# A two-block network on one core: the first norm's transfers, angles and table loads put in another order

## The reference, cut to what matters

```python
def layer_norm(x, g, b):
    xf = x.astype(jnp.float32)
    mu = jnp.mean(xf, axis=-1, keepdims=True)
    var = jnp.mean(jnp.square(xf - mu), axis=-1, keepdims=True)
    return ((xf - mu) * lax.rsqrt(var + EPS) * g.astype(jnp.float32) + b.astype(jnp.float32)).astype(x.dtype)

def rope_tables(positions):
    inv = ROPE_BASE ** (-jnp.arange(0, MLA_ROPE, 2, dtype=jnp.float32) / MLA_ROPE)
    ang = positions.astype(jnp.float32)[..., None] * inv
    return jnp.cos(ang), jnp.sin(ang)

def first_block(x, positions, ln_in_g, ln_in_b, w_in, ...):
    cos, sin = rope_tables(positions)
    h = layer_norm(x, ln_in_g, ln_in_b)
    for l in range(DEPTH):
        mix = token_mixers(h, cos, sin, w_in[l], ...)
        ...
```

## Time and profile before

| what | value |
|---|---|
| median of 3 runs | 3002.48 us |
| profiled execution, own time | 3005.76 us |
| its span in the profile | 3003.8 us |
| TensorE busy | 2892.7 us (96%) |
| VectorE busy | 1781.0 us (59%) |
| ScalarE busy | 1444.2 us (48%) |
| GpSimd busy | 1127.0 us (38%) |
| granted TensorE clock, mean | 0.991 |

### The profile page before, as it was taken

How to read it: one execution, slowest core, us unless ns; L and a number is a source line. 1 busy time by engine, 2 the same in 40 slices (tenths; PEclk the granted TensorE clock), 3 DMA queues, 4 the chain that set the end, 5 groups by cost and what they waited for, 6 DMA issues and landing times.

```text
span 3003.8 us, 45876 instructions
## 1 busy us (share of the span) xinstructions
PE 2892.7 (96%) x13808; PEld 2341.6 (78%) x13808; DVE 1781.0 (59%) x2643; ACT 1444.2 (48%) x2178; POOL 1127.0 (38%) x667
## 2 busy tenths in 40 slices
PE   6999999999999999999999998999999999989998
PEld 5777888887778888877877877888768877877886
DVE  4785444035865442158644268999566643379997
ACT  3544555225554553212445135888323453238886
POOL 2323444543232444555643531111556444601102
PEclk9999999999999999999999998999999999999999
DMA  4213333532122334434322357999633222459997
GB/s 130 71 43 92 98 93 96 174 90 79 43 96 77 96 95 139 145 108 107 105 71 57 92 181 266 396 411 402 158 101 113 75 64 76 151 188 374 409 411 240
DMA packets 374724, 466.55 MB, mean 155 GB/s; under 512 B 31334, under 2 KB 278176, under 8 KB 374496
## 3 DMA queue, kind: packets, MB, share of 16 engines
q1 hardware_dynamic: 349712, 391.52, 38.6%
q0 software_dynamic: 14944, 53.01, 5.4%
q10 hardware_dynamic: 9840, 19.29, 2.2%
HBM read 423.09 MB, written 33.55 MB: 152 GB/s over the span
## 4 chain that ended last, share of the span: by engine, by line
PE 58%; issue 22%; POOL 9%; DVE 6%; ACT 2%; ACTq 1%; DMA 1%; POOLq 0%; DVEq 0%; SPq 0%
PE bank L489 8%; PE bank L490 8%; POOL unit_lo L409 7%; PE bank L2207 4%; PE bank L2360 3%; PE bank L2361 3%; PE bank L2364 3%; PE bank L848 2%; PE bank L2374 2%; PE bank L2375 2%; PE bank L2378 2%; PE bank L1037 2%; PE bank L953 1%; PE bank L956 1%; PE bank L954 1%
## 5 line engine op out<-in xcount | busy, mean ns | idle before, releaser
L409 POOL TENSOR_TENSOR unit_lo<-unit_raw,unit_hi 128x1024 fp32r<-128x1024 f32 (+1 forms) x186 | 444.9, 2395 | 738.6 <-ACT unit_hi L402 738.6
L489 PE MATMUL bank<-xT_hi,unit_hi 128*128 128x512 f32 (+1 forms) x1776 | 689.5, 392 | 8.1 <-DVE d_lo L2875 3.7
L490 PE MATMUL bank<-xT_lo,unit_hi 128*128 128x512 f32 (+1 forms) x1776 | 667.2, 380 | 0.0
L489 PEld LDWEIGHTS bank<-xT_hi,unit_hi 128*128 128x128 f32 x1776 | 335.8, 189 | 95.7 <-issue 26.0
L490 PEld LDWEIGHTS bank<-xT_lo,unit_hi 128*128 128x128 f32 x1776 | 336.2, 189 | 64.5 <-issue 5.6
L402 ACT ACTIVATE unit_hi<-unit_raw 128x1024 fp32r<-128x1024 f32 (+1 forms) x186 | 194.8, 1047 | 367.0 <-PE bank L848 152.9
L394 POOL TENSOR_TENSOR unit_lo<-unit_raw,unit_hi 128x1024 fp32r<-128x1024 f32 (+2 forms) x158 | 325.3, 2059 | 13.2
L392 POOL TENSOR_SCALAR unit_hi<-unit_raw 128x1024 fp32r<-128x1024 f32 (+2 forms) x158 | 150.3, 951 | 459.6 <-PE bank L2207 269.4
L474 DVE TENSOR_TENSOR wt_lo<-wt,wt_hi 128x1024 fp32r<-128x1024 f32 x192 | 238.5, 1269 | 33.8 <-ACT wt_hi L469 33.0
L848 PE MATMUL bank<-xT_hi,unit_lo 128*128 128x512 f32 x976 | 241.2, 389 | 0.0
L474 DVE TENSOR_TENSOR xT_lo<-wt,xT_hi 128x1024 fp32r<-128x1024 f32 x192 | 233.1, 1219 | 8.3 <-ACT xT_hi L469 0.8
(11 more groups left out here) (585 smaller groups left out, 6206.2 us busy)
## 6 DMA issues: line engine op xcount, KB each, us to landing
wt<-in_w SPq DMA_DIRECT2D x384, 512.0 KB, 7.2
unit_raw<-in_w_in SPq DMA_DIRECT2D x272, 256.0 KB, 3.1
unit_raw<-in_w_ffn_up SPq DMA_DIRECT2D x176, 256.0 KB, 3.1
unit_raw<-in_w_ffn_down SPq DMA_DIRECT2D x88, 256.0 KB, 3.0
unit_raw<-in_w_out SPq DMA_DIRECT2D x64, 256.0 KB, 2.8
y_rows<-yb POOLq DMA_DIRECT2D x28, 512.0 KB, 7.1
y_rows<-zeros POOLq DMA_DIRECT2D x24, 512.0 KB, 5.2
unit_raw<-in_w_br SPq DMA_DIRECT2D x96, 128.0 KB, 2.3
```

The source lines that it names most:

```text
L409: pool.eng.tensor_tensor(lo, raw, hi.bitcast(F32), SUB).then_inc(self.split, 1)
L489: pe.matmul(out, wh, xh, start=first, stop=False)
L490: pe.matmul(out, wh, xl, start=False, stop=False)
```

## The change

On SyncE's queue, row tile 0 comes first, then g and b, then tile 1, the bulk of `konst`, the turning matrix, and tiles 2 and 3. The positions and the frequencies move to ScalarE's queue. The angles are computed by GpSimd instead of VectorE, with instructions of one or two inputs (12 of them, each waiting for the one before). ScalarE takes the square root of a constant first, which loads the square root's table. The sine stands behind the high part of tile 0 and the tables behind the high part of tile 1 in ScalarE's list. TensorE's list is the same.

```diff
@@ -100,7 +100,7 @@
     "ld_turn": (2, 0, 0),
     "ld_x": (1, 0, 0),
     "tab_mm": (4, 0, 0),
-    "tab_ev": (4, 0, 0),
+    "tab_ev": (5, 0, 0),
     "h_st": (0, 0, 4),
     "ov_wt": (0, 0, 48),
     "ov_x": (0, 0, 8),
@@ -108,7 +108,7 @@
     "ov_read": (0, 0, 32),
     "ov_val": (0, 0, 128),
     "ov_begin": (2, 0, 16),
-    "set_up": (7, 0, 0),
+    "set_up": (18, 0, 0),
     "y_zero": (0, 12, 0),
     "xb_ld": (0, 0, 16),
     "y_st": (0, 0, 14),
@@ -187,7 +187,7 @@
     "h_hi": (0, 0, 17),
     "y_ev": (0, 0, 33),
     "gt_use": (0, 0, 26),
-    "v_step": (24, 236, 342),
+    "v_step": (16, 236, 342),
     "norm_var": (4, 8, 8),
     "norm_z": (4, 8, 8),
     "norm_lo": (8, 16, 16),
@@ -778,13 +778,12 @@
                 high(NT - 1)
                 return
             deviation(0)
-            beside[0]()
             for i in range(NT):
                 if i + 1 < NT:
                     deviation(i + 1)
                 high(i)
-                if i == 1:
-                    beside[1]()
+                if i < 2:
+                    beside[i]()
 
         LAST = -NT
 
@@ -3157,17 +3156,13 @@
 
         def loads0(E):
             sp = E.eng
-            posi = proj[0:N_ANGLES, 0, :].bitcast(I32)
-            for rows, name in ((slice(0, 32), "positions"), (slice(32, N_ANGLES), "positions_2")):
-                sp.dma_start(posi[rows, :], over(t[name], [rows.stop - rows.start, S])).then_inc(ld.sem, ld.up(E))
-            sp.dma_start(konst[:, K_FREQ:K_END], t["konst"][:, K_FREQ:K_END]).then_inc(ld.sem, ld.up(E))
-
             def x_tile(i):
                 sp.dma_start(h[:, i, :], x_rows[:, i, :]).then_inc(x_there[i].sem, x_there[i].up(E))
 
             x_tile(0)
+            load_gb(E, t["ln_in_g"].rearrange("(o n) -> o n", o=1), t["ln_in_b"].rearrange("(o n) -> o n", o=1))
+            x_tile(1)
             sp.dma_start(konst[:, 0:K_FREQ], t["konst"][:, 0:K_FREQ]).then_inc(ld_turn.sem, ld_turn.up(E))
-            x_tile(1)
             sp.dma_start(proj[0:N_ANGLES, 3, :], t["konst"][0:N_ANGLES, K_TURN:N_KONST]).then_inc(ld_turn.sem, ld_turn.up(E))
             x_tile(2)
             x_tile(3)
@@ -3187,6 +3182,25 @@
             feed.prime(g, None)
             for _ in range(2):
                 g.nop().then_inc(ov_begin.sem, ov_begin.up(G))
+            ang, cyc, whole, arg = (proj[0:N_ANGLES, k, :] for k in (1, 2, 4, 5))
+            freq, quarter, half_pi = (konst[0:N_ANGLES, K_FREQ + k:K_FREQ + k + 1] for k in range(3))
+            G.eng.wait_ge(ld.sem, ld.at(G, 3))
+            g.tensor_copy(ang, proj[0:N_ANGLES, 0, :].bitcast(I32)).then_inc(set_up.sem, set_up.up(G))
+            G.eng.wait_ge(set_up.sem, set_up.last(G))
+            g.tensor_scalar(ang, ang, freq, None, MUL).then_inc(set_up.sem, set_up.up(G))
+            G.eng.wait_ge(set_up.sem, set_up.last(G))
+            g.tensor_scalar(cyc, ang, 1.0 / TWO_PI, quarter, MUL, ADD).then_inc(set_up.sem, set_up.up(G))
+            G.eng.wait_ge(set_up.sem, set_up.last(G))
+            g.tensor_scalar(cyc, cyc, MAGIC, MAGIC, ADD, SUB).then_inc(set_up.sem, set_up.up(G))
+            G.eng.wait_ge(set_up.sem, set_up.last(G))
+            for n, part in enumerate((C1, C2, C3)):
+                g.tensor_scalar(whole, cyc, -part, None, MUL).then_inc(set_up.sem, set_up.up(G))
+                G.eng.wait_ge(set_up.sem, set_up.last(G))
+                g.tensor_tensor(arg, whole, arg if n else ang, ADD).then_inc(set_up.sem, set_up.up(G))
+                G.eng.wait_ge(set_up.sem, set_up.last(G))
+            g.tensor_scalar(arg, arg, half_pi, PI_BELOW, ADD, MIN).then_inc(set_up.sem, set_up.up(G))
+            G.eng.wait_ge(set_up.sem, set_up.last(G))
+            g.tensor_scalar(arg, arg, -PI_BELOW, None, MAX).then_inc(tab_arg.sem, tab_arg.up(G))
 
         def tensor0(T):
             ring.prime(None, T.eng)
@@ -3199,11 +3213,16 @@
             T.eng.wait_ge(tab_sin.sem, tab_sin.at(T, 1))
             for n in range(4):
                 T.eng.matmul(bank[4 + n][:], proj[0:N_ANGLES, 3, n * P:n * P + P], proj[0:N_ANGLES, 4, :], start=True, stop=True).then_inc(tab_mm.sem, tab_mm.up(T))
-            T.eng.wait_ge(tab_ev.sem, tab_ev.at(T, 4))
+            T.eng.wait_ge(tab_ev.sem, tab_ev.at(T, 5))
 
         def scalar0(A):
-            load_gb(A, t["ln_in_g"].rearrange("(o n) -> o n", o=1), t["ln_in_b"].rearrange("(o n) -> o n", o=1))
+            act = A.eng
+            posi = proj[0:N_ANGLES, 0, :].bitcast(I32)
+            for rows, name in ((slice(0, 32), "positions"), (slice(32, N_ANGLES), "positions_2")):
+                act.dma_start(posi[rows, :], over(t[name], [rows.stop - rows.start, S])).then_inc(ld.sem, ld.up(A))
+            act.dma_start(konst[:, K_FREQ:K_END], t["konst"][:, K_FREQ:K_END]).then_inc(ld.sem, ld.up(A))
             A.eng.wait_ge(set_up.sem, set_up.at(A, 7))
+            act.activation(small[:, 2:3], eps, ACT.Sqrt).then_inc(tab_ev.sem, tab_ev.up(A))
 
             def sines():
                 A.eng.wait_ge(tab_arg.sem, tab_arg.at(A, 1))
@@ -3220,31 +3239,12 @@
         def vector0(V):
             v = V.eng
             v.nop().then_inc(up_lo.sem, up_lo.up(V))
-            V.eng.wait_ge(ld.sem, ld.at(V, 3))
-            V.eng.wait_ge(set_up.sem, set_up.at(V, 7))
-            ang, cyc, arg = (proj[0:N_ANGLES, k, :] for k in (1, 2, 5))
-            freq, quarter, half_pi = (konst[0:N_ANGLES, K_FREQ + k:K_FREQ + k + 1] for k in range(3))
-            v.tensor_copy(ang, proj[0:N_ANGLES, 0, :].bitcast(I32)).then_inc(v_step.sem, v_step.up(V))
-            V.eng.wait_ge(v_step.sem, v_step.last(V))
-            v.tensor_scalar(ang, ang, freq, None, MUL).then_inc(v_step.sem, v_step.up(V))
-            V.eng.wait_ge(v_step.sem, v_step.last(V))
-            v.tensor_scalar(cyc, ang, 1.0 / TWO_PI, quarter, MUL, ADD).then_inc(v_step.sem, v_step.up(V))
-            V.eng.wait_ge(v_step.sem, v_step.last(V))
-            v.tensor_scalar(cyc, cyc, MAGIC, MAGIC, ADD, SUB).then_inc(v_step.sem, v_step.up(V))
-            V.eng.wait_ge(v_step.sem, v_step.last(V))
-            for n, part in enumerate((C1, C2, C3)):
-                v.scalar_tensor_tensor(arg, cyc, -part, arg if n else ang, MUL, ADD).then_inc(v_step.sem, v_step.up(V))
-                V.eng.wait_ge(v_step.sem, v_step.last(V))
-
             def first():
                 V.eng.wait_ge(x_there[0].sem, x_there[0].at(V, 1))
                 for x in range(2):
                     v.bn_stats(stats[:, 0, x, :], h[:, 0, x * S:x * S + S]).then_inc(v_step.sem, v_step.up(V))
                 V.eng.wait_ge(v_step.sem, v_step.last(V))
                 v.bn_aggr(mv[:, 0, :], flat(stats[:, 0, :, :])).then_inc(norm_var.sem, norm_var.up(V))
-                v.tensor_scalar(arg, arg, half_pi, PI_BELOW, ADD, MIN).then_inc(v_step.sem, v_step.up(V))
-                V.eng.wait_ge(v_step.sem, v_step.last(V))
-                v.tensor_scalar(arg, arg, -PI_BELOW, None, MAX).then_inc(tab_arg.sem, tab_arg.up(V))
                 V.eng.wait_ge(gb_ld.sem, gb_ld.at(V, 2))
 
             norm_v(V, 0, None, first=first)
```

## The result

| | before | changed |
|---|---|---|
| median | 3002.48 us (3000.89 to 3006.58, 9 runs) | 3011.24 us (3008.07 to 3013.25, 9 runs) |
| profiled execution, own time | 3005.76 us | 3013.24 us |
| its span | 3003.8 us | 3011.6 us |
| norm of tile 2 done (the mark) | 32.09 us | 38.08 us |
| transposes of tile 2, duration | 1.09 us | 1.97 us |

The ratio is 1.0026, with an interval of 1.0017 to 1.0035: some 8.8 us or 0.3% slower, and outside the range that was given. The median forecast was 3001.5 us.

What follows compares the result with a forecast made beforehand. TensorE's start bounds it, through tile 2's norm at 32.09 us. Landing 7.0 + angles 10.4 + waiting 4.4 = 21.8, plus 9.3 gives 31.1: 1.0 earlier, so 3002.48 becomes 3001.5 us, range 2997.0 to 3006.5.

Steps and rivals of the forecast that it cites:

- Their landing is not shown ... I take 7.0: Positions and frequencies on ScalarE's queue: landing assumed at 7.0 us, bounded by 5.2 and 9.0.
- Nine of one input at 0.70: Angles on GpSimd: nine one-input instructions make 6.3 us, part of 10.4 us for all twelve.
- The bound, 16.3: Upper bound for the twelve angle instructions if one-input ones cost a TENSOR_TENSOR: 16.3 us instead of 10.4, mark +5.9.
- I add 4 x 1.1 = 4.4 us: Waiting added to GpSimd's angles because four two-input VectorE instructions of tiles 0 and 1 fall beside them: 4.4 us.
- they alternate: Claim that GpSimd and VectorE, on two-input VectorE work, take turns, each waiting for the other; 1.1 us per meeting.
- From the angles to this mark it is 9.3 us: From the angles' end at 21.8 us, via sine and tile 1, to tile 2's norm at 31.1 us: 9.3 us.
- So I cost it at nothing: Transfer order behind g and b: same number of issues ahead of the first weight unit on SyncE's queue, cost nothing.
- The clock: Rival, chance 0.30: TensorE idles about 3 us before tile 2's transposes, its clock falls, 2.3 us lost; 3003.8 us.
- slower by over 0.2%: Outcome given chance 0.05, said to need late angles and a fallen clock together.
- Late angles: Rival, chance 0.05: cast and factors on GpSimd cost like two-input work, angles +5.9 us, mark 4.9 later; 3007.4 us.
- Code to load: Rival, chance 0.03: GpSimd stops at the configuration instruction between cast and first multiplication; 3007.4 us, or 3006.5 to 3007.5.
- Early angles: Rival, chance 0.12: positions land at 5.2 us on their own queue, angles done at 17.8, gain 5.0; 2997.5 us.

Runs made afterwards that it cites:

- four rewritten instructions: Changed kernel with four single multiplications of the angles on GpSimd written as multiply-and-add of zero; median 3010.3 us, ratio 1.0019 to the kernel before.
- all pairs rewritten: Four multiplications as multiply-and-add, plus add-subtract and add-minimum-maximum split into multiply-and-adds and a minimum-and-maximum, against the changed kernel; 3004.03 us, one execution.
- GpSimd at its best: Kernel before with preloaded table, g and b behind it on ScalarE's queue, 13 cheap-form angle instructions on GpSimd, sine behind tile 0's high part; 3003.66 us, ratio 0.9998.
- queue order alone: Kernel before with only the transfers put in the change's order; median 3004.66 us, ratio 1.0011.
- the sine in its old place: Changed kernel with the sine back ahead of tile 1's deviation, angles still on GpSimd; 3013.51 us, one execution.
- the vectors behind the preload: Kernel before with the square root's table preloaded and g and b issued behind it on ScalarE's queue; median 2998.94 us, ratio 0.9987.
- the idle products: Changed kernel with three unread products of 512 columns on TensorE before tile 2's transposes; median 3012.76 us, ratio 1.0031 to the kernel before.

## Why the prediction was wrong

The mark was predicted at 31.1 us and came at 38.08. The 7.0 us between them come from the angles: done at 29.15 instead of 21.8.

- **"Their landing is not shown ... I take 7.0"**: the frequencies were there at 9.7, 2.7 later and outside the bound of 9.0. The bound assumed that the whole set is there when it was before; on this queue the small transfers came last.
- **"Nine of one input at 0.70"** failed, and it is the largest miss. The rows of GpSimd's TENSOR_SCALAR had one form only, and I priced the others like it: L392 is written `tensor_scalar(hi, raw, 1.0, 0.0, MUL, ADD)` in `part`, a multiply-and-add, and of the nine only L3192 is one. By the prices without a collision (cast 0.61, L3190 1.57, L3192 0.68, L3194 1.95, three pairs of 1.49 + 1.26, then 2.00 and 1.49, with eleven gaps of 0.08) the angles take 17.4 us, not 10.4: +7.0. The four rewritten instructions (1.50 to 0.62, 1.57 to 0.68) show that the form is the cause. L3190's 1.57 is no collision as far as can be told: its column of factors costs some 0.07 among the multiply-and-adds too (0.68 or 0.69 against 0.62). The bound, 16.3, was also too low.
- **"I add 4 x 1.1 = 4.4 us"** was too much for these forms. 19.42 us were measured, so collisions cost 2.0 of them: 0.8 on the cast, 1.0 on L3194 and 0.2 on L3192 and the gaps, while all four of VectorE's instructions of two inputs did fall into this stretch (9.38 to 16.45 us). That is -2.4. The second of the four ran beside the single-step L3190 from 11.81 to 12.79 us and took its usual 1.27, so "they alternate" does not hold for every form. Where the forms are the cheap ones it does, and nearly with this price: with all pairs rewritten the same four meetings cost GpSimd 3.3 us, and with GpSimd at its best 3.4. The landing, the forms and the meetings together are +7.3.
- **"From the angles to this mark it is 9.3 us"** held: 8.9. So did what stands in it: VectorE waiting for tile 1's high part, tile 1's norm finished by 18 (16.45), tile 0's transfer there near 5.2 (5.75), and a preloaded table whose gain is spent in waiting.
- **"So I cost it at nothing"**, of the transfers behind g and b, held as far as the weight units go: with the queue order alone they start at 17.14 us against 17.22. What the new order cost, 3.2 us on the mark when alone, came through the landing above and through the meetings that followed from it.
- **The clock** (0.30) came in and cost 2.5 where 2.3 were predicted. It counted only together with the late angles, which is the pair that "slower by over 0.2%" (0.05) named. That chance was too low: the sum rested on a form that stood in one row, and on a landing that stood in none.
- **Late angles** (0.05), priced at +5.9 on the angles for unseen forms, came nearest, and the forms alone were worth 7.0. But it looked for the price in the cast and in the factors, which cost 0.61 and some 0.07; what cost were the single steps and the pairs of an addition with a subtraction or a minimum. **Code to load** (0.03) did not happen: the cast ends at 11.11 and the first multiplication starts at 11.22. **Early angles** (0.12) had the landing the wrong way round.

The statement of the GPSIMD Engine Reference of the Trainium skill (Engine selection), that one-input work runs at roughly line rate there, holds for some forms only. VectorE takes 0.42 to 0.48 us for these instructions; GpSimd took 0.61 to 0.73 for a cast, a multiply-and-add and a minimum-and-maximum, but 1.49 for a single step and 1.95 to 2.00 for an addition followed by a subtraction or a minimum.

## What to carry to other kernels

Before a chain of dependent instructions is moved to another engine, look for each form (both steps, the kind of operand) in that engine's rows; where a form has no row, its price is open by a factor of three (0.62 to 2.0 here), and the chance of a loss should say so. Small transfers that start a chain should be issued ahead of the large ones on the other queues too, since a queue of their own did not protect them here. An engine that has room (GpSimd was 38% busy) is no reason to give it a chain that a later stage waits for: its 19.4 us replaced 5.1 on VectorE.

## What the runs showed that I had not expected

- **A form's price on GpSimd.** For 96 x 512 numbers 0.62 us as a multiply-and-add, 1.49 as a multiplication alone: adding a zero made it faster by 0.9 us, in four instructions of one kernel. An addition and subtraction without a collision took 1.95, in this row of the kernel with the sine in its old place (GpSimd's timeline):

```profile
13.54 1.95 POOL L3195 TENSOR_SCALAR proj<-proj 96x512 f32<-96x512 f32 x1
```

- **Small transfers behind large ones.** The same 63 KB took 7.6, 5.6 and 4.6 us to land, as the other queue held tile 0, g, b and more, then g and b, then g and b issued 0.9 us later. No run moves the small ones to their own queue without moving the large ones ahead, so the two are not told apart.
- **What stays open.** Pauses of 2.76, 2.66, 2.15 and 2.02 us in front of tile 2's transposes went with a fallen clock in the changed kernel and in the one with other forms. So did one of 1.62 us with GpSimd at its best, but one of 2.72 in the kernel with the vectors behind the preload did not, nor one of 1.49 with all pairs rewritten. TensorE's timelines of the 1.62 and the 2.72:

```profile
30.45 1.52 PE L795 MATMUL bank<-konst,h 128*128 128x128 f32 x8 [1.62 <-DVE h L710]
```

```profile
29.83 1.10 PE L796 MATMUL bank<-konst,h 128*128 128x128 f32 x8 [2.72 <-DVE h L710]
```

The length of the pause alone does not decide it, and what does is not settled here.

Nor do the medians resolve 1 to 3 us. In the kernel with the queue order alone the transposes that stand at 1288.95 us before came 3.7 later and those at 2140.01 only 0.3 later. In between lie the experts, where the DMA share is 0.95 from 1800 to 2100 us in both kernels. This is one trace of each kernel, so that the executions scatter there by some 3 us is likely and not shown. It would explain why the gain of 1.8 us from the idle products, and the 2.7 from the forms, are seen in the traces and not in the medians.
